# Mixture of experts with streamed weights: shared blocks put into the line of routed blocks, and the shared weights' place reused as a fifth place of the ring

## What is computed

```
scores = sigmoid(h @ w_router)                 # 64 experts, the best 6 of 4 groups of 8 chosen
wts    = chosen scores / their sum * 2.5
hid_e  = silu(h @ w1[e]) * (h @ w3[e])         # 1024 -> 256
routed = sum over the 6 chosen of wts * (hid_e @ w2[e])
shared = (silu(h @ ws1) * (h @ ws3)) @ ws2     # one more expert of the same size, for every token
x      = x + gate * (routed + shared)          # then a final RMSNorm
```

## Time and profile before

| what | value |
|---|---|
| median of 3 runs (lowest, highest) | 1673.31 us (1669.88, 1674.69) |
| profiled execution: its time, its span | 1673.73 us, 1671.9 us |
| PE busy | 1465.8 us, 88% of the span |
| DVE, POOL, ACT busy | 847.5, 468.0, 222.0 us |
| moved by the DMA engines | 365.36 MB, of it 55.40 MB by POOL's queue |
| mean granted clock of TensorE | 0.931 |

### The profile page before, as it was taken

How to read it: one execution, slowest core, us unless ns; L and a number is a source line. 1 busy time by engine, 2 the same in 40 slices (tenths; PEclk the granted TensorE clock), 3 DMA queues, 4 the chain that set the end, 5 groups by cost and what they waited for, 6 DMA issues and landing times.

```text
span 1671.9 us, 18471 instructions
## 1 busy us (share of the span) xinstructions
PE 1465.8 (88%) x5851; PEld 662.7 (40%) x5851; DVE 847.5 (51%) x2134; ACT 222.0 (13%) x365; POOL 468.0 (28%) x495
## 2 busy tenths in 40 slices
PE   4899999999999999886989996897888999688947
PEld 2444544455544545543433342342222333233313
DVE  1156878899898986655333332233232333232317
ACT  1112121321212222111100000000000000000003
POOL 0001011111121212113024554344452555443510
PEclk7999999999999999576999998998989999798988
DMA  9985111101110115141766999898998999898976
GB/s 335 335 327 184 66 54 38 53 28 64 54 38 5 39 40 166 45 108 52 251 215 231 368 366 351 314 366 305 364 369 295 365 373 365 278 380 303 366 241 246
DMA packets 96738, 365.36 MB, mean 219 GB/s; under 512 B 17427, under 2 KB 33719, under 8 KB 71581
## 3 DMA queue, kind: packets, MB, share of 16 engines
q1 hardware_dynamic: 75717, 308.98, 48.5%
q0 software_dynamic: 20944, 55.40, 13.2%
HBM read 318.35 MB, written 57.41 MB: 225 GB/s over the span
## 4 chain that ended last, share of the span: by engine, by line
PE 48%; DVE 19%; DMA 19%; issue 8%; SPq 4%; ACT 1%; POOL 0%; POOLq 0%; DVEq 0%; ACTq 0%
PE U L838 18%; PE U L656 8%; PE R L854 8%; DVE cv L1196 8%; DMA acc_rows<-xr,slot_cur 7%; PE R L709 7%; DMA acc_rows<-W,slot_cur 6%; DMA W<-in_w 2%; SPq L373 2%; DMA W<-in_w_ada 1%; DMA W<-h_rows,tok_cur 1%; PE R L620 1%; PE T L844 1%; PE T L673 1%; PE U L680 1%
## 5 line engine op out<-in xcount | busy, mean ns | idle before, releaser
L656 PE MATMUL U<-W,hT 128*128 128x512 f32 x864 | 384.5, 599 | 1.2 <-issue 1.2
L838 PE MATMUL U<-W,cat 128*32 128x512 f32 (+2 forms) x912 | 249.1, 648 | 46.6 <-issue 30.3
L838 PE MATMUL U<-W,hT 128*32 128x512 f32 (+2 forms) x1136 | 247.9, 631 | 33.3 <-issue 28.8
L1196 DVE SCALAR_TENSOR_TENSOR cv<-win,cw,cv 128x128 f32<-128x128 f32 x960 | 254.9, 345 | 1.4
L854 PE MATMUL R<-W,glu 128*32 128x512 f32 (+2 forms) x1024 | 240.7, 596 | 2.7 <-DVE glu L1461 2.7
L656 PEld LDWEIGHTS U<-W,hT 128*128 128x128 f32 x864 | 162.2, 193 | 187.5 <-issue 187.5
L838 PEld LDWEIGHTS U<-W,cat 128*32 128x32 f32 (+2 forms) x912 | 92.1, 155 | 180.5 <-issue 168.0
L838 PEld LDWEIGHTS U<-W,hT 128*32 128x32 f32 (+2 forms) x1136 | 87.8, 140 | 169.3 <-issue 163.0
L854 PEld LDWEIGHTS R<-W,glu 128*32 128x32 f32 (+2 forms) x1024 | 84.4, 138 | 151.0 <-issue 147.9
L1674 POOL DMA_INDIRECT x_t<-h_rows,tok_cur x116 | 118.0, 1017 | 53.5 <-issue 27.0
L1090 ACT ACTIVATE sg<-U 128x256 f32<-128x256 f32 x66 | 25.3, 384 | 789.8 <-PE U L838 789.8
(11 more groups left out here) (250 smaller groups left out, 1212.4 us busy)
## 6 DMA issues: line engine op xcount, KB each, us to landing
W<-in_w SPq DMA_DIRECT2D x192, 1024.0 KB, 12.4
W<-in_w_ada SPq DMA_DIRECT2D x24, 1024.0 KB, 9.3
W<-in_w_in SPq DMA_DIRECT2D x6, 2048.0 KB, 19.9
W<-acc_rows SPq DMA_DIRECT2D x16, 512.0 KB, 9.8
x_rows<-xr SPq DMA_DIRECT2D x9, 512.0 KB, 3.3
h_rows<-xr SPq DMA_DIRECT2D x9, 512.0 KB, 2.7
x_t<-in_x_prompt SPq DMA_DIRECT2D x8, 512.0 KB
W<-in_w_out SPq DMA_DIRECT2D x1, 4096.0 KB, 17.7
```

What stands on the lines that cost most here:

```text
L656: last = mm(U[BANK[g]][:, :], hT[:, k, :], w_in[:, k, 512 * g:512 * g + 512], start=k == 0, stop=k == KT - 1)
L838: last = mm(U[1][cols, :], xgT[z][:, k, cols], w13[:, :, k, :], start=k == 0, stop=k == KT - 1)
L1196: ins = v.scalar_tensor_tensor(cv[:, c, :], win[:, c, w:w + P], cw[:, c, w:w + 1], cv[:, c, :], ALU.mult, ALU.add)
```

## The change

- **One line of blocks.** `EXEC` puts the 66 blocks in one order: shared blocks 0 to 4, then units 0 to 3 each followed by one of the shared blocks 5 to 8, then units 4 to 56. A position in this line is x = 0 to 65. All semaphore counts follow x.
- **Unit order.** `even_order` counts the four interleaved shared blocks, so the units come in another order: the line now begins with four units of two experts each.
- **Shared rows by POOL.** The nine shared blocks' rows are gathered by POOL's indirect DMAs and their results added to `acc_rows` by indirect accumulating DMAs, with constant indices (`shared_at`, one more constant to load, and one conversion on DVE). The plain loads and stores on SP are gone, with the waits of the routed part for them. `acc_rows` is filled with zeros in both halves (ten fills of 1 MB instead of five) during the mixer, and one small fill (line 512) goes.
- **Five places.** When the last shared block is done (x = 12), `shw` is a fifth place. Each expert takes the place that comes free first (`SLOT`), and `FREE[s]` is the position after which SP may load it. The last eight experts use four places only, as `shw` is needed for the residual rows at the end.
- **Loops written out.** POOL, DVE and ACT have every block written out; POOL's DMAs take their indices straight from `tok_qb` and `slot_i`, without the copies into `tok_cur` and `slot_cur`.

```diff
+NX = NT + NU
+EXEC = [(None, n) for n in range(AHEAD)]
+for u in range(NU):
+    EXEC += [(u, None)] + [(None, AHEAD + u)] * (AHEAD + u < NT)
+LAST = tuple(max(AT[n // 4] for n, (x, _) in enumerate(QUARTERS) if x == s) for s in range(NE))
+SLOT, FREE, free = [], [], [-1] * RING + [max(x for x, (u, _) in enumerate(EXEC) if u is None)]
+for s in range(NE):
+    r = min(range(RING + (s < NE - 8)), key=lambda x: free[x])
+    SLOT.append(r)
+    FREE.append(free[r])
+    free[r] = LAST[s]
...
-        ring = W[:, WE:(RING + 1) * WE].rearrange("p (r w) -> p r w", r=RING)
+        ring = [W[:, WE * (r + 1):WE * (r + 2)] for r in range(RING)] + [shw]
...
-                sp.dma_start(acc_rows[bass.ds(i * 2 * P + TABLE - 4 * P, 2 * P), :], t["zeros"]).then_inc(spare_in, 16)
+                for x in range(2):
+                    sp.dma_start(acc_rows[bass.ds(i * 2 * P + TABLE * x - 4 * P, 2 * P), :], t["zeros"]).then_inc(spare_in, 16)
...
-                if s >= RING:
-                    sp.wait_ge(h_done, NT + last_unit[s - RING] + 1)
-                load_up(e, s % RING, 0)
-                load_up(e, s % RING, 1)
-                if s >= RING:
-                    sp.wait_ge(y_done, NT + last_unit[s - RING] + 1)
-                load_down(e, s % RING)
-
-            for n in range(1, 3):
-                load_rows((n + 2) // 2, n % 2)
-                store_shared(n - 1)
+                if FREE[s] >= 0:
+                    sp.wait_ge(h_done, FREE[s] + 1)
+                load_up(e, SLOT[s], 0)
+                load_up(e, SLOT[s], 1)
+                if FREE[s] >= 0:
+                    sp.wait_ge(y_done, FREE[s] + 1)
+                load_down(e, SLOT[s])
+
             sp.wait_ge(line_ready, 1)
-            for n in range(3, NT + 1):
-                if n <= NT - 3:
-                    load_rows((n + 2) // 2, n % 2)
-                if n < RING + 3:
-                    load_in_line(n - 3)
-                store_shared(n - 1)
-            for s in range(RING, NE):
+            for s in range(NE):
                 load_in_line(s)
...
-            dve.wait_ge(ysh_stored, 16 * NT)
...
+            def gather(x):
+                u, n = EXEC[x]
+                pool.wait_ge(xgT_ready, floor(x - 1))
+                ...
+                for q in range(4):
+                    pool.indirect_dma_start(xgs[x % 2][:, QW * q:QW * q + QW], None, rows, ...)
+
+            def scatter(x):
+                u, n = EXEC[x]
+                at = shared_i[:, 4 * NT + n:4 * NT + n + 1] if u is None else slot_i[:, u:u + 1]
+                pool.wait_ge(y_evac, x + 1)
+                if x > 0:
+                    pool.wait_ge(scattered[1 - x % 2], 16 * ((x + 1) // 2))
+                pool.indirect_dma_start(acc_rows, ..., compute_op=ALU.add).then_inc(scattered[x % 2], 16)
...
+            scatter(0)
+            gather(4)
+            scatter(1)
+            pool.wait_ge(slot_ready, 2)
+            for x in range(2, NX):
+                if x + 3 < NX:
+                    gather(x + 3)
+                scatter(x)
```

More of the change, by code:

```diff
@@ L58, in even_order, with beside @@
 def even_order(made):
-    pace = sum(units_of(x) for x in made) / NE
+    pace = (sum(units_of(x) for x in made) + NT - AHEAD) / NE
     order, units, experts = [], 0, 0
+    def beside(n):
+        return n + min(n, NT - AHEAD)
     while made:
-        best = min(made, key=lambda x: abs(units + units_of(x) - pace * (experts + len(x))))
+        best = min(made, key=lambda x: abs(beside(units + units_of(x)) - pace * (experts + len(x))))
         made.remove(best)
@@ L79 @@
 TABLE = 10 * P
+NX = NT + NU
+EXEC = [(None, n) for n in range(AHEAD)]
+for u in range(NU):
+    EXEC += [(u, None)] + [(None, AHEAD + u)] * (AHEAD + u < NT)
+AT = {u: x for x, (u, n) in enumerate(EXEC) if u is not None}
+assert NX % 2 == 0 and len(EXEC) == NX
+LAST = tuple(max(AT[n // 4] for n, (x, _) in enumerate(QUARTERS) if x == s) for s in range(NE))
[5 more added lines that the diff above has]
+    free[r] = LAST[s]
+USE = tuple(SLOT[:s + 1].count(SLOT[s]) for s in range(NE))
 CAPS = tuple(32 * sum(x == s for x, _ in QUARTERS) for s in range(NE))
@@ L82 @@
 LCAP = -(-(max(CAPS) + P * ROUNDS) // 32) * 32
-RING = 4
 SW = D * NS // P
@@ L893, in _, with parts_of @@
             rank_products()
-            for n in range(2, NT):
-                up(n, shw_all, n % 2)
-                down(n - 1, shw_all)
-                hidden_trans(n)
-                if n == 2:
-                    spread_lists()
-                if n == 3:
-                    pe.wait_ge(rounds_posed, 1)
-                    mm(U[0][0:1, 0:NE], rounds_c[0:NE, :], ident[0:NE, 0:NE], start=True, stop=True).then_inc(rounds_posed, 1)
-            down(NT - 1, shw_all)
-            def parts_of(u):
+            def parts_of(x):
+                u = EXEC[x][0]
+                if u is None:
+                    return shw_all
                 parts = []
@@ L1096, in _ @@
             score(TP)
-            with act.Fori(1, NT) as n:
-                blk_silu(n)
-            with act.Fori(0, NU) as u:
-                blk_silu(u + NT)
+            for x in range(1, NX):
+                blk_silu(x)
             act.wait_ge(rounds_known, 1)
@@ L1504, in _ @@
             dve.wait_ge(rank_ready, 1)
-            shared(1)
+            block(1)
             dve.wait_ge(rank_posed, 1)
@@ L1511, in _ @@
             dve.wait_ge(line_ready, 1)
-            shared(2)
+            block(2)
             dve.wait_ge(slot_posed, 1)
@@ L1526, in _ @@
             v.tensor_reduce(rounds_c[0:NE, :], over[0:NE, :], AX.X, ALU.add).then_inc(rounds_posed, 1)
-            shared(3)
+            block(3)
             dve.wait_ge(rounds_posed, 2)
@@ L1530, in _ @@
             v.tensor_copy(rounds_i, rounds_f).then_inc(rounds_known, 1)
-            for n in range(4, NT - 1):
-                shared(n)
-            shared(NT - 1)
-            shared_y(NT - 1)
-            dve.wait_ge(ysh_stored, 16 * NT)
-            def routed(g, r, first=False, last=False):
-                b = 2 * g + r
-                if r == 0 and not last:
-                    xpose(b + NT + 1, NT % 2 ^ 1, 1, gathered[1], 64 * g + 64)
-                elif r == 1:
-                    xpose(b + NT + 1, NT % 2, 0, gathered[0], 64 * g + 128)
-                blk_hid(b + NT)
-                if not first:
-                    if r == 0:
-                        blk_y(b - 1, scattered[1], 16 * g - 16, 1)
-                    else:
-                        blk_y(b - 1, scattered[0], 16 * g, 0)
-                blk_hidT(b + NT)
-            xpose(NT, NT % 2, 0, gathered[0], 64)
-            routed(0, 0, True)
-            routed(0, 1)
-            routed(1, 0)
-            routed(1, 1)
-            with dve.Fori(2, NU // 2) as g:
-                routed(g, 0)
-                routed(g, 1)
-            routed(NU // 2, 0, last=True)
-            blk_y(NU - 1, scattered[0], 16 * (NU // 2), 0)
+            for x in range(4, NX):
+                block(x)
+            blk_y(NX - 1)
             dve.wait_ge(rounds_known, 1)
@@ L1704, in _ @@
-            scatter(NU // 2 - 1, 0)
-            scatter(NU // 2 - 1, 1)
-            scatter(NU // 2, 0)
+            pool.wait_ge(spare_in, 16 * 10)
+            scatter(0)
+            gather(4)
+            scatter(1)
+            pool.wait_ge(slot_ready, 2)
+            for x in range(2, NX):
+                if x + 3 < NX:
+                    gather(x + 3)
+                scatter(x)
             pool.wait_ge(rounds_known, 1)
```

218 lines of the change are left out of this document (103 added, 115 removed).

## The result

The changed kernel takes **1590.34 us** (median of 4 runs, 1588.74 to 1591.95), the kernel before 1672.47 (4 runs, 1669.88 to 1674.69). The ratio is 0.9509, with a 95% interval of 0.9492 to 0.9527. The forecast was 1605 us, with a range of 1586 to 1642. It had the sign and the main mechanism right and was 15 us too slow.

A forecast was written before the change was run, and what follows sets the result against it. The DMA engines were taken to bound the stage, with 107 us of their time lost. Regaining 16.9 at the start, 16 at the changeover and 35.2 in dips gave 68 us: 1605 us, range 1586 to 1642.

The forecast's parts named there:

- The bound: From experts' names known to last scatter's landing: DMA engines move 268.5 MB, 728 us at 369 GB/s; 106 us unused.
- The start of the stage: The moment when the experts' names are known, read from the kernel before as 787.9.
- Loads start at once: SP's first expert load, near 788 without shared transfers ahead: all 16.9 us lost before 840 regained.
- The changeover: From shared blocks to units, gap at 840 to 900: 16 us lost where 32 were; bounds 5 and 32.
- The dips: Five dips between 1040 and 1540: the fifth place cuts 45.2 us lost to 10; bounds 0 and 45.
- Nine shared blocks through POOL: Shared blocks' scatters in place of plain stores: cost taken as 0, up to 102 us if the scatter line decides.
- The sum: Whole stage: 39 us DMA time lost instead of 107, gain 68 us, last scatter at 1554, time 1605 us.
- the forecast's own case: Whole kernel: the forecast of 1605 us with its own range 1591 to 1624, chance 0.66.
- All gaps close: Rival for start and dips: no dips, line of scatters ends last at 1538, time 1590 us; chance 0.08.
- The dips stay: Rival: the wait of PE and SP on each other is only moved, gain 33 us, time 1640; chance 0.18.
- The lines for a slower kernel: Rival in POOL's queue: scatters become the bound, the change loses from links of 12.62 us; chance 0.04.
- What would show it: Signs: first load near 788, DMA share near 1.03 from 852 to 1530, last landing near 1554, links 11.3 us.

The follow-up runs named there:

- the three kernels that undo halves: Changed kernel with four places only, 1619.72 us; with all nine shared blocks ahead of the first unit, 1611.27 us; with both, 1649.53 us.
- both halves undone: Changed kernel with four places only and all nine shared blocks ahead of the first unit: 1649.53 us, ratio 0.9884 to the kernel before.
- the one with the store alone: Kernel before, with the last prompt block's x and h stores moved ahead of the shared-block loads on SP: 1664.7 us, ratio 0.998.

## Why the prediction was right, and where it was off

- **The bound.** "DMA time not used" was the right quantity: the three kernels that undo halves lose 26, 22 and 57 us more of it and take 29, 21 and 59 us longer, and taking bytes away gives 36 us where taking the scatters' waits away gives some 4. The rate of the earlier trace rows carried: 365 GB/s over 658 us. The Trainium skill (DMA: Bandwidth & Descriptors, Specifications) gives some 358 GB/s as a core's share; this stretch, too, lies above it.
- **The start of the stage, the first step that failed.** The forecast read the stage "from the moment when the experts' names are known, 787.9", and took that moment as given. It is 780.5 now, 7.4 us earlier in the two profiled runs (5.2 in the second trace of the changed kernel). That the plain loads on SP are gone was followed only behind 787.9, but it also frees the store of x, which stood behind them at 745.81. The row with DVE's 4.57 us of waiting was in the trace of before. The store by itself gave 3 to 4 us in its experiment.
- **Loads start at once, 16.9 us.** Right, as far as the runs part it: the kernel with both halves undone is 16 us faster than the one with the store alone. Of the 16.9 us lost in these two stretches 4.1 are left before 840; the 2.9 of them behind 805 are counted in the next term.
- **The changeover, the second step that was mis-sized.** Forecast: 16 us lost, bounds 5 and 32. Measured: 2.9 + 2.6 = 5.5 us from 805 to 900, near the lower bound. The fifth expert goes at 825.93. The forecast's 838 less the earlier start of 7 us is 831, and the 5 us allowed for late lists are not in the trace: 826. The four places are full at 781.65 + 44 = 826 by the forecast's own count, so the 6 us of empty engines did not occur. The wait for w2 behind it came as described (14 us, to 840.08), but with transfers in flight.
- **The dips, 45 to 10 us.** Right in kind and size. In four of the five former places together under 1 us is lost, in the whole middle some 7. Without the fifth place the time is 29 us longer; the forecast had 35.
- **Nine shared blocks through POOL, 0.** Not contradicted: the kernel with both halves undone shows no cost.
- **The sum.** The forecast's stage is 834 - 68 = 766 us from 788 on; it takes 757.35 us from 781.65 on. So 8.6 us of the miss are the shorter stage (by the account lost DMA time is 29 us, not 39: 9 less at the start, 3 less in the middle, 1 more at the end; the rates are rounded to 1 GB/s) and 6.4 the earlier first load. These 15 us are the miss: 1590.34 lies in the whole range, 1586 to 1642, but just under the range of the forecast's own case, 1591 to 1624.
- **The rivals.** "All gaps close" gave 1590 to the microsecond, and its sum for the line of scatters, 1538, is the landing that was measured (1538.79). But its reason does not hold: the line ends last, yet without it the kernel gains only some 4 us. What spoke for it, that from 1295 to 1425 nothing but scatters held the chain, was misread: in the trace of before they hold it to 1397, and then come a gather and PE. The agreement is partly luck, as the first scatter starts at 785.8 and not at 795, links are 11.23 and not 11.33 us, and three gathers break the line on the chain, at 873, 943 and 1163. "The dips stay" describes the kernel with four places: that one took 1620, and the rival's 1640 less the two misses at the start, 7 and 9 us, is 1624. The lines for a slower kernel needed links of 12.62 us; they got shorter.
- **What would show it.** The share of about 1.03 from 852 on (1.02 to 1510), no stretch like 840 to 900, links of 11.3 us (11.23) and the long but harmless wait for y_done came as announced; the first load (788, was 781.65) and the last landing (1554, was 1538.8) came earlier.

## What to carry to other kernels

Where transfers feed a stage, add up the DMA time that is not used, stretch by stretch, and ask of each gap who fails to ask for data there. A place in a ring is worth the idle time of the gaps that it closes, and here two gaps of different cause needed two different edits: undoing one costs 29 us, the other 21, both together 59. When transfers are taken off a queue, follow what stood behind them also in the stage before: a store that leaves earlier can move the start of everything. And a line that fills the chain of waits need not be the bound: take its waits away, and take load off what it waits on, before working on it.

## What the runs showed of the hardware that was not expected

- An accumulating scatter of 0.5 MB landed in 10.4 us among engines at 369 GB/s. Over the scatters on the chain from 975 on the mean was 10.2 us in the changed kernel (365 GB/s in its middle), and still 9.8 us with half of w2 left out (338 GB/s). It was 6.0 to 6.5 us where much less moved: at the very end (1532.59, above), and for the four scatters that start between 832 and 864 in the kernel with all shared blocks first, around its gap of 97 GB/s. So from 369 down to 338 GB/s its price hardly changed; it fell where the engines ran dry.
- A DMA share of 1.00 stood beside 338 GB/s in that run, where 1.02 and 1.03 stood beside 365 and 369 GB/s. The share counts the time that packets take, and here it did not tell that PE had become the bound; PE's own busy time (626.5 of 630 us) did.
- Small list writes that had to land before a read were waited for 5.55 us instead of 1.93 us when the first weight loads were asked for 4.3 us earlier, counted from the same step of DVE (35.6 us behind it instead of 40.0).
